# Seven half-size products for the gate, up and input tiles of a two-block transformer kernel, with the feed-forward values on token rows

## The chip, the cores and the metric

The kernel runs on one core of a Trainium2 chip. The metric is the device time of one execution in microseconds (us). TensorE (PE) multiplies matrices from SBUF into PSUM banks, VectorE (DVE) and ScalarE (ACT) work on the results, and SyncE (SP) issues the loads of weights. All data are fp32.

## The reference

256 tokens of width 1024 pass a first block (a Hyena and mLSTM mixer, then a 16-expert feed-forward) and two layers of a second block. The change is only in the second block, in these lines:

```
h = rms_norm(x, norm_mix[l]) * (1.0 + sc_m) + sh_m
(q_a, kc_a, ..., v_b, g_br) = jnp.split(h @ w_in[l], split_at, axis=-1)
...
h = rms_norm(x, norm_ffn[l]) * (1.0 + sc_f) + sh_f
gt, up = jnp.split(h @ w_ffn_in[l], 2, axis=-1)
x = x + g_f * ((jax.nn.silu(gt) * up) @ w_ffn_out[l])
```

`w_in` is 1024 x 4888, of which the first 2840 columns are projected to token rows; `w_ffn_in` is 1024 x 5632 (gate and up, 2816 each), `w_ffn_out` 2816 x 1024.

## The kernel before

The program is written out by hand, one instruction stream per engine, with semaphores between them. `step(name)` counts a finished instruction, `wait_ge(*at(name))` waits for it. Weights come as a stream of tiles, 128 partitions x 4096 floats (2 MB: 1024 rows x 512 columns), into a ring of four slots; the tile four places on is loaded as soon as TensorE has used the slot (`mark_used`, `one`). Six PSUM banks of 512 columns rotate (`bank`); a claim waits until the bank's last content is read.

Activations `h2` stand turned, channels on partitions: 8 blocks of 128 channels x 256 tokens. Two forms of a linear layer use them. `pe_linear_tok` (L837) holds 128 tokens of `h2` as the stationary side and streams 512 weight columns, 8 matmuls for each half of the tokens, so the result has tokens on partitions; the input projection `pe_in` uses it for six tiles (five of 512 columns, one of 280), and ScalarE copies each bank to `qkv` (`act_in`, L1826). `pe_linear_T` (L823) holds 128 weight columns and streams the 256 tokens, 8 matmuls for each of 4 column blocks, so the result stands turned. The feed-forward `pe_ffn` uses it for six gate and six up tiles (the sixth has 256 columns); ScalarE applies SiLU to gate banks (`act_ffn`, L2362), VectorE multiplies with up (`dve_ffn`, L2375) into `ffT`, which the down projection (L2342, 176 matmuls) streams.

A layer of the second block is, on TensorE: norm, `pe_late` (a vector product with two tiles of the next ada matrix, L633), `pe_in`, `pe_compress` with gate matmuls, attention, the mixer's output (L1375, then L823), norm, `pe_late`, `pe_ffn`. On VectorE, the norm's scaling (L744; L802 and L808 at the first layer, where two norms are joined) goes ahead of what the layer needs.

## Time and profile before

| | us |
|---|---|
| median of 3 runs | 2339.05 (2338.96 to 2340.21) |
| profiled execution | 2338.81 |
| its span, first to last instruction | 2337.0 |
| TensorE busy | 1974.4 (84%) |
| VectorE busy | 414.0 (18%) |
| ScalarE busy | 319.6 (14%) |

A busy share is an average over stages with different limits: the expert loop in the middle third waits for weights from HBM. The chain of waits says, for each moment, which work the end depended on. The trace holds two TensorE records for each fp32 matmul and one for a transpose.

### The profile page before, as it was taken

How to read it: one execution, taken by the hardware profiler on the slowest of the kernel's cores; microseconds unless marked ns; L12 is line 12 of the kernel's file. 1: busy time of each engine (PE TensorE's matmuls, PEld its weight loads, DVE VectorE, ACT ScalarE, POOL GpSimd, SP SyncE). 2: the span in 40 equal slices, each digit the busy share in tenths (PEclk: the TensorE clock that was granted, in tenths of full speed). 3: DMA queues.
4: the chain of work that ended last, by engine and by line, in shares of the span. 5: the costliest groups of instructions: out<-in, count | busy, mean ns of one | idle time of the engine just before them, and what ended most of it. 6: DMA issues, size and time to landing. Idle time of an engine off the chain costs nothing.

```text
span 2337.0 us, 27864 instructions
## 1 busy us (share of the span) xinstructions
PE 1974.4 (84%) x12006; PEld 1244.0 (53%) x12006; DVE 414.0 (18%) x1223; ACT 319.6 (14%) x724; POOL 0.2 (0%) x4
## 2 busy tenths in 40 slices
PE   7999999966666666666666689999999999999999
PEld 4468678521111111111111155878888748688888
DVE  5113334300000000000000032551000106620000
ACT  3132030200000000000000022341000103510000
POOL 0000000000000000000000000000000000000000
PEclk9999999988787888877788799999999999999999
DMA  9146568999999999999999973526434545255341
GB/s 350 71 147 221 208 241 307 403 428 428 429 428 429 428 429 428 429 428 429 428 429 429 429 283 129 210 80 234 162 108 162 200 162 198 85 187 188 119 180 36
DMA packets 147871, 648.45 MB, mean 277 GB/s; under 512 B 10645, under 2 KB 17410, under 8 KB 123016
## 3 DMA queue, kind: packets, MB, share of 16 engines
q1 hardware_dynamic: 143956, 643.74, 69.6%
q10 hardware_dynamic: 3828, 3.43, 0.5%
q8 instruction: 69, 1.13, 0.2%
q14 instruction: 18, 0.15, 0.0%
HBM read 646.10 MB, written 1.05 MB: 277 GB/s over the span
## 4 chain that ended last, share of the span: by engine, by line
PE 61%; DMA 33%; DVE 3%; ACT 1%; issue 1%; SPq 1%; ACTq 0%; DVEq 0%
DMA ring<-in_w_exp 32%; PE bank L823 26%; PE bank L837 7%; PE bank L2342 7%; PE bank L1623 4%; PE bank L1375 4%; PE bank L2302 2%; PE bank L1638 2%; PE bank L856 1%; DMA ring<-in_w_ada 1%; PE bank L593 1%; DVE scr L2213 1%; PE bank L633 1%; PE bank L1300 1%; PE bank L701 1%
## 5 line engine op out<-in xcount | busy, mean ns | idle before, releaser
L823 PE MATMUL bank<-hx,ring 128*128 128x256 f32 (+1 forms) x2688 | 600.0, 386 | 0.7 <-ACT hx L719 0.7
L823 PEld LDWEIGHTS bank<-hx,ring 128*128 128x128 f32 x2688 | 512.2, 191 | 86.9 <-issue 19.1
L1623 PE MATMUL bank<-ring,arena 128*32 128x512 f32 x1968 | 307.5, 759 | 203.0 <-DMA ring<-in_w_exp 192.6
L1623 PEld LDWEIGHTS bank<-ring,arena 128*32 128x32 f32 x1968 | 61.1, 124 | 432.7 <-DMA ring<-in_w_exp 312.6
L1638 PE MATMUL bank<-ring,arena 128*32 128x512 f32 x1008 | 162.6, 785 | 80.9 <-DMA ring<-in_w_exp 70.1
L2342 PE MATMUL bank<-arena,ring 128*128 128x256 f32 x704 | 152.4, 379 | 1.5 <-DVE arena L2375 1.5
L837 PE MATMUL bank<-ring,hx 128*128 128x512 f32 (+1 forms) x384 | 152.9, 561 | 0.7 <-ACT hx L779 0.7
L2342 PEld LDWEIGHTS bank<-arena,ring 128*128 128x128 f32 x704 | 133.7, 190 | 20.0 <-issue 1.9
L1638 PEld LDWEIGHTS bank<-ring,arena 128*32 128x32 f32 x1008 | 32.5, 131 | 194.3 <-DMA ring<-in_w_exp 114.6
L837 PEld LDWEIGHTS bank<-ring,hx 128*128 128x128 f32 x384 | 72.8, 190 | 79.6 <-issue 75.3
L1681 DVE COPY arena<-bank 128x256 f32<-128x256 f32 x16 | 6.8, 424 | 519.0 <-PE bank L1628 519.0
L1375 PE MATMUL bank<-arena,ring 128*128 128x256 f32 x384 | 85.3, 385 | 2.1 <-DVE arena L1264 2.1
L1375 PEld LDWEIGHTS bank<-arena,ring 128*128 128x128 f32 x384 | 73.9, 193 | 13.0 <-issue 2.7
L1688 DVE COPY arena<-bank 128x256 f32<-128x256 f32 x16 | 6.8, 424 | 348.5 <-PE bank L1512 348.5
L2375 DVE TENSOR_TENSOR arena<-bank,scr 128x512 f32<-128x512 f32 x22 | 15.2, 691 | 286.5 <-PE bank L823 286.5
L1646 PE MATMUL bank<-arena 128*128 128x256 f32 x256 | 59.8, 387 | 5.2 <-ACT arena L1667 5.2
L1646 PEld LDWEIGHTS bank<-arena 128*128 128x128 f32 x256 | 47.6, 191 | 19.6 <-issue 13.0
L2302 PE MATMUL bank<-hx,ring 128*128 128x256 f32 x256 | 57.3, 382 | 0.0
L1663 ACT COPY arena<-bank 128x512 f32<-128x512 f32 x16 | 9.4, 585 | 348.3 <-PE bank L1631 348.3
L2302 PEld LDWEIGHTS bank<-hx,ring 128*128 128x128 f32 x256 | 48.0, 190 | 8.2 <-issue 1.8
L2362 ACT ACTIVATE scr<-bank 128x512 f32<-128x512 f32 x22 | 13.1, 597 | 261.7 <-PE bank L823 261.6
L1661 ACT ACTIVATE arena<-bank 128x512 f32<-128x512 f32 x16 | 9.6, 597 | 279.0 <-PE bank L1623 279.0
(375 smaller groups left out, 1418.9 us busy)
## 6 DMA issues: line engine op xcount, KB each, us to landing
ring<-in_w_exp SPq DMA_DIRECT2D x186, 2048.0 KB, 16.2
ring<-in_w_ada SPq DMA_DIRECT2D x36, 2048.0 KB, 12.4
ring<-in_w_in SPq DMA_DIRECT2D x29, 2048.0 KB, 9.1
...
```

Source lines behind the costliest of these rows:

```text
L593: ins = pe.matmul(banks[6][32 * j:32 * j + 32, (i % 4) * P:(i % 4 + 1) * P], cT[:, k, :], w[:, k, j * P:(j + 1) * P], start=k == 0, stop=k ...
L633: ins = pe.matmul(b[32 * j:32 * j + 32, i * P:(i + 1) * P], cT[:, k, :], w[:, k, j * P:(j + 1) * P], start=k == 0, stop=k == KD - 1)
L701: ins = pe.matmul(b[:, 0:n], ones[:, 0:P], sq[:, k, :], start=k == 0, stop=k == KD - 1)
L823: ins = pe.matmul(b[:, o:o + n], w[:, k, j * P:(j + 1) * P], h[:, k, :], start=k == 0, stop=k == KD - 1)
L837: ins = pe.matmul(b[:, 0:n], h[:, k, c * P:(c + 1) * P], w[:, k, :], start=k == 0, stop=k == KD - 1)
L856: pe.matmul(b[:, :], hcx[:, k, s * N + c * P:s * N + (c + 1) * P], w[:, k, :], start=k == 0, stop=False)
L1375: ins = pe.matmul(b[:, s * N:(s + 1) * N], w[:, k, j * P:(j + 1) * P], y[:, k, :], start=k == 0, stop=k == 3)
L1623: ins = pe.matmul(banks[s][32 * j:32 * j + 32, :], e_xe[:, 2 * t + kk, :], w[:, kk, 512 * j:512 * j + 512], start=t + kk == 0, stop=t + kk ...
L1638: ins = pe.matmul(banks[half][32 * k:32 * k + 32, :], e_hT[:, k, 32 * t:32 * t + 32], w[:, k, 512 * half:512 * half + 512], start=t == 0, ...
L1646: ins = pe.matmul(banks[4 + j // 2][:, (j % 2) * N:(j % 2 + 1) * N], e_y[:, j * P:(j + 1) * P], e_G, start=False, stop=True, skip_group_ch ...
L2302: ins = pe.matmul(b[:, j * N:(j + 1) * N], w[:, k, (2 * i + j) * P:(2 * i + j + 1) * P], h2[:, k, :], start=k == 0, stop=k == KD - 1)
L2342: ins = pe.matmul(acc[j // 2][:, (j % 2) * N:(j % 2 + 1) * N], w[:, k, j * P:(j + 1) * P], ffT[:, f, :], start=f == 0 and j % 2 == 0, stop ...
```

## The change

A product of the 256 x 1024 activations with a 1024 x 512 weight tile is split in halves three ways (tokens, channels, columns). Instead of eight half-size products it makes seven, by the scheme of Winograd and Strassen: four sums of weight quarters (T1 to T4, VectorE, 128 x 1024 each, for every tile), four sums of activation parts (S1 to S4, once a layer for each use), seven products of 4 matmuls of 256 columns, and additions of the results (u2, u3, c22, c21, c12 on VectorE; a copy of m1 and of c11 on ScalarE). Tokens are on partitions in the result. This is done for input tiles 1, 3, 4 and 5 and for gate and up tiles 0 to 4 of each layer. In the feed-forward SiLU and product are made on token rows (`gtok`, `htok`), and eight transposes for each tile pair turn them for the down projection. The sixth, small pair of tiles keeps the old form and comes first.

```diff
@@ -291,7 +291,7 @@
         late_tiles(3 * l + 2)
         wf = A["w_ffn_in_2"][l]
         gt, up = wide(wf, 0, FF2), wide(wf, FF2, 2 * FF2)
-        for i in range(len(gt)):
+        for i in (5, 0, 1, 2, 3, 4):
             tiles2(f"gt{l}_{i}_", gt[i:i + 1])
             tiles2(f"up{l}_{i}_", up[i:i + 1])
         tiles2(f"down{l}_", deep(A["w_ffn_out_2"][l], 0, FF2))
@@ -1811,7 +1811,130 @@
     def pe_in(pe, l):
         PE.stage("second")
         for t in range(6):
-            pe_linear_tok(pe, f"in{l}_{t}", f"in{l}_{t}", h2, None if t else f"h mix{l + 1}")
+            if t in SEVEN:
+                pe_seven(pe, f"in{l}_{t}", f"in{l}_{t}", SEVEN.index(t) % 2, f"S in{l}")
+            else:
+                pe_linear_tok(pe, f"in{l}_{t}", f"in{l}_{t}", h2, None if t else f"h mix{l + 1}")
+
+    SEVEN = (1, 3, 4, 5)
+    tsum = view(arena, 7088, P, 2, 4, 1024)
+    ssum = view(arena, 15280, P, 4, 4, P)
+    m1, u2, u3 = scr[:, 2048:2304], scr[:, 2304:2560], scr[:, 2560:2816]
+
+    def quarter(w, kh, nh):
+        return w[:, 4 * kh:4 * kh + 4, 256 * nh:256 * nh + 256]
+
+    def part(th, kh):
+        return h2[:, 4 * kh:4 * kh + 4, th * P:(th + 1) * P]
+
+    def tsums(half):
+        return [tsum[:, half, i].rearrange("p (k n) -> p k n", k=4) for i in range(4)]
+
+    def pe_seven(pe, key, tkey, half, s_ready, between=None):
+        w = tile(pe, tkey)
+        T1, T2, T3, T4 = tsums(half)
+        S1, S2, S3, S4 = (ssum[:, i] for i in range(4))
+
+        def product(name, b, a, x, first):
+            for k in range(4):
+                ins = pe.matmul(b[:, 0:256], a[:, k, :], x[:, k, :], start=first and k == 0, stop=True, skip_group_check=True)
+            ins.then_inc(*PE.step(f"{name} {key}"))
+
+        r1 = bank(pe, f"{key}r1")
+        product("m1", r1, part(0, 0), quarter(w, 0, 0), True)
+        pe.wait_ge(*at(f"T2 {key}"))
+        pe.wait_ge(*at(s_ready))
+        r2 = bank(pe, f"{key}r2")
+        product("m6", r2, S2, T2, True)
+        if between:
+            between()
+        r3 = bank(pe, f"{key}r3")
+        product("m5", r3, S1, T1, True)
+        pe.wait_ge(*at(f"u2 {key}"))
+        product("m7", r2, S3, T3, False)
+        pe.wait_ge(*at(f"m1 copied {key}"))
+        product("m2", r1, part(0, 1), quarter(w, 1, 0), False)
+        pe.wait_ge(*at(f"T4 {key}"))
+        pe.wait_ge(*at(f"u3 {key}"))
+        product("m4", r2, part(1, 1), T4, False)
+        pe.wait_ge(*at(f"c22 {key}"))
+        product("m3", r3, S4, quarter(w, 1, 1), False)
+        mark_used(pe, tkey)
+
+    def dve_tsum(v, key, tkey, half, two_back, i):
+        w = tile(v, tkey)
+        T1, T2, T3, T4 = tsums(half)
+        if i == 0:
+            if two_back:
+                v.wait_ge(*at(f"m3 {two_back}"))
+            v.tensor_tensor(T1, quarter(w, 0, 1), quarter(w, 0, 0), ALU.subtract).then_inc(*DV.step(f"T1 {key}"))
+        elif i == 1:
+            v.tensor_tensor(T3, quarter(w, 1, 1), quarter(w, 0, 1), ALU.subtract).then_inc(*DV.step())
+        elif i == 2:
+            v.wait_ge(*at(f"T1 {key}"))
+            v.tensor_tensor(T2, quarter(w, 1, 1), T1, ALU.subtract).then_inc(*DV.step(f"T2 {key}"))
+        else:
+            v.wait_ge(*at(f"T2 {key}"))
+            v.tensor_tensor(T4, quarter(w, 1, 0), T2, ALU.subtract).then_inc(*DV.step(f"T4 {key}"))
+
+    def dve_ssum(v, ready, name):
+        v.wait_ge(*at(ready))
+        S1, S2, S3, S4 = (ssum[:, i] for i in range(4))
+        v.tensor_tensor(S1, part(1, 0), part(1, 1), ALU.add).then_inc(*DV.step())
+        s1 = DV.last()
+        v.tensor_tensor(S3, part(0, 0), part(1, 0), ALU.subtract).then_inc(*DV.step())
+        v.wait_ge(*s1)
+        v.tensor_tensor(S2, S1, part(0, 0), ALU.subtract).then_inc(*DV.step())
+        v.wait_ge(*DV.last())
+        v.tensor_tensor(S4, part(0, 1), S2, ALU.subtract).then_inc(*DV.step(name))
+
+    def dve_seven(v, key, tkey, half, after, before, out, gate=None):
+        b1, b2, b3 = (bank_of(f"{key}r{i}")[:, 0:256] for i in (1, 2, 3))
+
+        def gated(c, h):
+            if gate is not None:
+                v.wait_ge(*DV.last())
+                x = out(c, h)
+                v.tensor_tensor(x, x, gate[:, c, 256 * h:256 * h + 256], ALU.mult).then_inc(*DV.step(f"{key} gated"))
+
+        v.wait_ge(*at(f"m1 copied {key}"))
+        v.wait_ge(*at(f"m6 {key}"))
+        if before:
+            v.wait_ge(*at(f"{before} sums"))
+        v.tensor_tensor(u2, b2, m1, ALU.add).then_inc(*DV.step(f"u2 {key}"))
+        if after:
+            dve_tsum(v, *after, 0)
+            dve_tsum(v, *after, 1)
+        v.wait_ge(*at(f"m7 {key}"))
+        v.tensor_tensor(u3, b2, m1, ALU.add).then_inc(*DV.step(f"u3 {key}"))
+        v.wait_ge(*at(f"m5 {key}"))
+        v.wait_ge(*at(f"u3 {key}"))
+        v.tensor_tensor(out(1, 1), b3, u3, ALU.add).then_inc(*DV.step(f"c22 {key}"))
+        gated(1, 1)
+        if after:
+            dve_tsum(v, *after, 2)
+        if gate is not None:
+            v.wait_ge(*at(f"m2 {key}"))
+            v.tensor_tensor(out(0, 0), b1, gate[:, 0, 0:256], ALU.mult).then_inc(*DV.step(f"free {key}r1", f"{key} gated"))
+        if after:
+            dve_tsum(v, *after, 3)
+        v.wait_ge(*at(f"m4 {key}"))
+        v.tensor_tensor(out(1, 0), b2, m1, ALU.add).then_inc(*DV.step(f"free {key}r2", f"c21 {key}"))
+        gated(1, 0)
+        v.wait_ge(*at(f"m3 {key}"))
+        v.tensor_tensor(out(0, 1), b3, u2, ALU.add).then_inc(*DV.step(f"free {key}r3", f"{key} sums"))
+        gated(0, 1)
+
+    def dve_in_tiles(v, l):
+        DV.stage("second")
+        todo = [(f"in{l}_{t}", f"in{l}_{t}", n % 2, f"in{l}_{SEVEN[n - 2]}" if n >= 2 else None) for n, t in enumerate(SEVEN)]
+        for i in range(4):
+            dve_tsum(v, *todo[0], i)
+        dve_ssum(v, f"h mix{l + 1} done", f"S in{l}")
+        for n, t in enumerate(SEVEN):
+            lo = IN_COLS[t][0]
+            dve_seven(v, *todo[n][:3], todo[n + 1] if n < 3 else None, todo[n - 1][0] if n else None,
+                      lambda c, h: qkv[:, c, lo + 256 * h:lo + 256 * h + 256])
 
@@ -1819,12 +1942,23 @@
         AC.stage("second")
         act.wait_ge(*at("x moe" if l == 0 else "ffn read0"))
         for t, (lo, hi) in enumerate(IN_COLS):
+            if t in SEVEN:
+                key = f"in{l}_{t}"
+                b = bank_of(f"{key}r1")[:, 0:256]
+                act.wait_ge(*at(f"m1 {key}"))
+                if t != SEVEN[0]:
+                    act.wait_ge(*at(f"c21 in{l}_{SEVEN[SEVEN.index(t) - 1]}"))
+                act.copy(m1, b).then_inc(*AC.step(f"m1 copied {key}"))
+                act.wait_ge(*at(f"m2 {key}"))
+                act.copy(qkv[:, 0, lo:lo + 256], b).then_inc(*AC.step(f"free {key}r1", f"in{l} {t}"))
+                continue
             for c in range(NC):
                 key = f"in{l}_{t}{c}"
                 act.wait_ge(*at("full " + key))
                 b = bank_of(key)
                 act.copy(qkv[:, c, lo:hi], b[:, 0:hi - lo]).then_inc(*AC.step("free " + key, f"in{l} {t}"))
         act.wait_ge(*AC.last())
+        act.wait_ge(*at(f"in{l}_5 sums"))
         for c in range(NC):
             for col, H, lo, _ in GROUPS:
                 act.activation(sqh[:, c, lo * HD:(lo + H) * HD], qkv[:, c, col:col + H * HD], ACT.Square).then_inc(*AC.step(f"squares{l}"))
@@ -1879,6 +2013,7 @@
 
         PE.stage("compress")
         pe.wait_ge(*at(f"in{l} 1"))
+        pe.wait_ge(*at(f"in{l}_1 sums"))
         pe.wait_ge(*at("pe ready"))
         for s in range(2):
             key = f"cturn{l}{s}"
@@ -2324,18 +2459,38 @@
                                            b[:, :].rearrange("p (j t) -> p j t", j=2), ACT.Sigmoid).then_inc(*AC.step("free " + key, f"gates{l + 1}"))
 
 
+    gtok = view(arena, 17328, P, NC, 512)
+    htok = view(arena, 18352, P, NC, 512)
+
+    def pe_hidden_turn(pe, l, i):
+        pe.wait_ge(*at(f"u{l}{i} gated"))
+        for h in range(2):
+            b = bank(pe, f"turn{l}{i}{h}")
+            for j in range(2):
+                for c in range(NC):
+                    o = (j * NC + c) * P
+                    q = (2 * h + j) * P
+                    ins = pe.transpose(b[:, o:o + P], htok[:, c, q:q + P], ident[:, :])
+            ins.then_inc(*PE.step(f"full turn{l}{i}{h}"))
+
     def pe_ffn(pe, l):
         PE.stage("ffn")
-        for i in range(6):
-            nb = 4 if i < 5 else 2
-            pe_linear_T(pe, f"g{l}{i}_", f"gt{l}_{i}_0", h2, N, nb, None if i else f"h ffn{l + 1}")
-            pe_linear_T(pe, f"u{l}{i}_", f"up{l}_{i}_0", h2, N, nb)
+        pe_linear_T(pe, f"g{l}5_", f"gt{l}_5_0", h2, N, 2, f"h ffn{l + 1}")
+        pe_linear_T(pe, f"u{l}5_", f"up{l}_5_0", h2, N, 2)
+        for i in range(5):
+            pe_seven(pe, f"g{l}{i}", f"gt{l}_{i}_0", 0, f"S ffn{l}", (lambda: pe_hidden_turn(pe, l, i - 1)) if i else None)
+            pe_seven(pe, f"u{l}{i}", f"up{l}_{i}_0", 1, f"S ffn{l}")
         pe_late_turn(pe, 3 * l + 2)
         acc = [bank(pe, f"down{l}{i}") for i in range(4)]
         pe.wait_ge(*at(f"hidden{l}"))
+        pe.wait_ge(*at(f"turned{l}3"))
         for t in range(6):
             w = tile(pe, f"down{l}_{t}")
             nk = 4 if t < 5 else 2
+            if t == 1:
+                pe_hidden_turn(pe, l, 4)
+            if t == 4:
+                pe.wait_ge(*at(f"turned{l}4"))
             for j in range(KD):
                 for k in range(nk):
                     f = 4 * t + k
@@ -2351,30 +2506,64 @@
     def act_ffn(act, l):
         AC.stage("ffn")
         act.wait_ge(*at(f"h ffn{l + 1} done"))
+        act.wait_ge(*at(f"full g{l}5_0"))
+        act.activation(sg[:, 0, :], bank_of(f"g{l}5_0")[:, :], ACT.Silu).then_inc(*AC.step(f"free g{l}5_0", f"sg{l}"))
+
+        def turns(i):
+            for h in range(2):
+                key = f"turn{l}{i}{h}"
                 act.wait_ge(*at("full " + key))
+                f = 4 * i + 2 * h
+                act.copy(ffT[:, f:f + 2, :].rearrange("p a b -> p (a b)"), bank_of(key)[:, :]).then_inc(
+                    *AC.step("free " + key, f"turned{l}{i}"))
+
+        for i in range(5):
+            for x in "gu":
+                key = f"{x}{l}{i}"
+                act.wait_ge(*at(f"m1 {key}"))
+                last = f"u{l}{i - 1}" if x == "g" else f"g{l}{i}"
+                if i or x == "u":
+                    act.wait_ge(*at(f"c21 {last}"))
+                b = bank_of(f"{key}r1")[:, 0:256]
+                act.copy(m1, b).then_inc(*AC.step(f"m1 copied {key}"))
+                if x == "u":
+                    continue
+                if i:
+                    turns(i - 1)
+                    act.wait_ge(*at(f"{last} gated"))
+                act.wait_ge(*at(f"m2 {key}"))
+                act.activation(gtok[:, 0, 0:256], b, ACT.Silu).then_inc(*AC.step(f"free {key}r1"))
+                act.wait_ge(*at(f"c21 {key}"))
+                act.activation(gtok[:, 1, :], gtok[:, 1, :], ACT.Silu).then_inc(*AC.step())
+                act.wait_ge(*at(f"{key} sums"))
+                act.activation(gtok[:, 0, 256:512], gtok[:, 0, 256:512], ACT.Silu).then_inc(*AC.step(f"silu{l}{i}"))
+        turns(4)
 
     def dve_ffn(v, l):
         DV.stage("ffn")
+        todo = []
+        for i in range(5):
+            for n, (x, w) in enumerate((("g", "gt"), ("u", "up"))):
+                todo.append((f"{x}{l}{i}", f"{w}{l}_{i}_0", n, f"{x}{l}{i - 1}" if i else None))
+        for i in range(4):
+            dve_tsum(v, *todo[0], i)
+        dve_ssum(v, f"h ffn{l + 1} done", f"S ffn{l}")
+        v.wait_ge(*at(f"full u{l}5_0"))
+        v.wait_ge(*at(f"sg{l}"))
+        v.tensor_tensor(ffT[:, 20:22, :].rearrange("p a b -> p (a b)"), bank_of(f"u{l}5_0")[:, :], sg[:, 0, :],
+                        ALU.mult).then_inc(*DV.step(f"free u{l}5_0", f"hidden{l}"))
+        for n, item in enumerate(todo):
+            i, up = n // 2, n % 2
+            after = todo[n + 1] if n + 1 < len(todo) else None
+            if up:
+                v.wait_ge(*at(f"silu{l}{i}"))
+                if i:
+                    v.wait_ge(*at(f"full turn{l}{i - 1}1"))
+            elif i:
+                v.wait_ge(*at(f"u{l}{i - 1} gated"))
+            dst = htok if up else gtok
+            dve_seven(v, *item[:3], after, todo[n - 1][0] if n else None,
+                      lambda c, h: dst[:, c, 256 * h:256 * h + 256], gtok if up else None)
         dve_late(v, 3 * l + 2)
         DV.stage("ffn")
         v.wait_ge(*at(f"ada21 part{3 * l + 2}"))
@@ -2525,6 +2714,7 @@
             if l == 0:
                 v.memset(kct, 0.0).then_inc(*DV.step())
                 v.memset(sC, 0.0).then_inc(*DV.step())
+            dve_in_tiles(v, l)
             dve_blocks(v, l)
             dve_late(v, 3 * l)
             dve_in(v, l)
```

TensorE's order in the feed-forward of a layer, from the late tiles' vector product to the norm that follows. Before:

```order
247 L633 MATMUL bank<-ring,small 32x128 x64
248 L823 MATMUL bank<-hx,ring 128x256 x352
249 L645 MATMUL bank<-ident,arena 128x128 x2
250 L2342 MATMUL bank<-arena,ring 128x256 x176
251 L701 MATMUL bank<-scr,ones 128x256 x8
```

Now, up to the first turn (L1840 is the product in `pe_seven`, L823 the small tiles; `hx` holds `h2`, `arena` the sums):

```order
267 L823 MATMUL bank<-hx,ring 128x256 x32
268 L1840 MATMUL bank<-ring,hx 128x256 x4
269 L1840 MATMUL bank<-arena 128x256 x12
270 L1840 MATMUL bank<-ring,hx 128x256 x4
271 L1840 MATMUL bank<-arena,hx 128x256 x4
272 L1840 MATMUL bank<-ring,arena 128x256 x4
273 L1840 MATMUL bank<-ring,hx 128x256 x4
274 L1840 MATMUL bank<-arena 128x256 x12
275 L1840 MATMUL bank<-ring,hx 128x256 x4
276 L1840 MATMUL bank<-arena,hx 128x256 x4
277 L1840 MATMUL bank<-ring,arena 128x256 x4
278 L1840 MATMUL bank<-ring,hx 128x256 x4
```

One run of 352 matmuls became 32 and then 28 for each of ten tiles; from the second pair on, 8 transposes (L2473) stand behind the gate tile's second product, and the last 8 behind 32 matmuls of the down projection.

VectorE's order at the first layer's input projection, from the end of the joined norm. Before:

```order
294 L2527 MEMSET arena 128x512
295 L1974 TENSOR_TENSOR hx<-bank,arena 64x256 x8
296 L661 TENSOR_TENSOR ada<-bank,cols 128x8
297 L1843 TENSOR_TENSOR arena<-arena 128x256
298 L1845 SCALAR_TENSOR_TENSOR arena<-arena 128x4x32
```

Now, up to the third result addition (L1870 to L1878 are T1, T3, T2, T4; L1883 to L1889 the activation sums; L1904 is u2, L1909 u3):

```order
294 L2716 MEMSET arena 128x512
295 L1870 TENSOR_TENSOR arena<-ring 128x1024
296 L1872 TENSOR_TENSOR arena<-ring 128x1024
297 L1875 TENSOR_TENSOR arena<-ring,arena 128x1024
298 L1878 TENSOR_TENSOR arena<-ring,arena 128x1024
299 L1883 TENSOR_TENSOR arena<-hx 128x512
300 L1885 TENSOR_TENSOR arena<-hx 128x512
301 L1887 TENSOR_TENSOR arena<-arena,hx 128x512
302 L1889 TENSOR_TENSOR arena<-hx,arena 128x512
303 L1904 TENSOR_TENSOR scr<-bank,scr 128x256
304 L1870 TENSOR_TENSOR arena<-ring 128x1024
305 L1872 TENSOR_TENSOR arena<-ring 128x1024
```

VectorE, which had nothing to do between the norm and the compression's block sums (L1974), has sums ahead of the first seven-product tile and the next tile's sums between the result additions.

## Rows read from the trace of the kernel before

**Rows 1.** the page, busy us of each engine, its share of the span, instructions
```profile
PE 1974.4 (84%) x12006; PEld 1244.0 (53%) x12006; DVE 414.0 (18%) x1223; ACT 319.6 (14%) x724; POOL 0.2 (0%) x4
```

**Rows 2.** the chain of waits in order of time: start us, us, what
```profile
1370.59 76.45 PE bank L837 x192
...
1617.53 152.20 PE bank L823 x704
...
1770.69 76.21 PE bank L2342 x352
...
1854.61 76.41 PE bank L837 x192
...
2100.82 152.20 PE bank L823 x704
```

**Rows 3.** busy us by stretch, instructions; then granted clock, DMA share, GB/s
```profile
core 0: us, PE busy (x) PEld busy (x) DVE busy (x) ACT busy (x) POOL busy (x), PEclk, DMA share, GB/s
450.00:1350.00 900.00, 584.33 (x3622) 171.00 (x3612) 39.55 (x93) 39.65 (x77) 0.00 (x0) 0.82 1.00 427
1488.00:1550.00 62.00, 57.91 (x425) 41.43 (x422) 41.33 (x207) 37.71 (x129) 0.00 (x0) 0.97 0.28 104
1972.00:2034.00 62.00, 57.15 (x428) 40.66 (x426) 41.41 (x207) 38.31 (x130) 0.00 (x0) 1.00 0.29 104
1617.00:1770.00 153.00, 152.59 (x714) 134.01 (x706) 9.77 (x18) 11.28 (x21) 0.00 (x0) 1.00 0.47 165
1371.00:1447.00 76.00, 76.00 (x194) 36.38 (x193) 7.25 (x16) 8.85 (x19) 0.00 (x0) 1.00 0.47 163
```

**Rows 4.** ScalarE in order of time in the first input projection
```profile
1384.60 0.58 ACT L1826 COPY arena<-bank 128x512 f32<-128x512 f32 x1 [6.23 <-PE bank L837]
1391.47 0.58 ACT L1826 COPY arena<-bank 128x512 f32<-128x512 f32 x1 [6.28 <-PE bank L837]
1398.33 0.58 ACT L1826 COPY arena<-bank 128x512 f32<-128x512 f32 x1 [6.28 <-PE bank L837]
```

**Rows 5.** TensorE's transposes of heads in order of time
```profile
1484.98 2.82 PE L2034 MATMUL bank<-ident,arena 128*128 128x128 f32 x24
1487.64 1.04 PE L2034 MATMUL bank<-ident,hx 128*128 128x128 f32 x8
```

**Rows 6.** TensorE at the first down projection, and the chain there
```profile
1770.69 76.21 PE L2342 MATMUL bank<-arena,ring 128*128 128x256 f32 x352 [0.76 <-DVE arena L2375]
...
1769.75 0.70 DVE arena L2375
1770.45 0.24 issue
```

**Rows 7.** VectorE and ScalarE by line and form: xcount | busy us, mean ns
```profile
L2375 DVE TENSOR_TENSOR arena<-bank,scr 128x512 f32<-128x512 f32 x22 | 15.2, 691 | 286.5 <-PE bank L823 286.5
...
L1864 DVE TENSOR_TENSOR arena<-arena 128x256 f32<-128x256 f32 x12 | 5.0, 416 | 0.1
...
L808 DVE SCALAR_TENSOR_TENSOR xT<-xT,cols,scr 128x256 f32<-128x256 f32 x8 | 3.3, 480 | 0.0
...
L494 DVE TENSOR_TENSOR arena<-mg 128x512 f32<-128x512 f32 x4 | 2.7, 686 | 0.0
...
L1256 DVE TENSOR_TENSOR arena<-arena,small 128x1024 f32<-128x1024 f32 x1 | 1.2, 1226 | 0.0
...
L2362 ACT ACTIVATE scr<-bank 128x512 f32<-128x512 f32 x22 | 13.1, 597 | 261.7 <-PE bank L823 261.6
...
L1941 ACT COPY arena<-bank 128x256 f32<-128x256 f32 x2 | 0.7, 372 | 2.7 <-PE bank L1903 2.7
```

**Rows 8.** TensorE where the second layer's gate tiles end, in order of time
```profile
1931.95 27.79 PE L823 MATMUL bank<-hx,ring 128*128 128x256 f32 x128
1959.67 1.09 PE L1903 MATMUL bank<-ring,hx 128*32 128x128 f32 x29
```

**Rows 9.** VectorE ahead of the first input projection's end, and at the second's start
```profile
1375.37 3.26 DVE L808 SCALAR_TENSOR_TENSOR xT<-xT,cols,scr 128x256 f32<-128x256 f32 x8
...
1378.75 0.48 DVE L2527 MEMSET arena<- 128x512 f32 x1
...
1853.16 3.26 DVE L744 SCALAR_TENSOR_TENSOR scr<-xT,small,rs 128x256 f32<-128x256 f32 x8
```

**Rows 10.** weight loads issued at the first feed-forward's start, and the queue's rate
```profile
1615.50 0.37 SPq L2554 DMA_DIRECT2D ring<-in_w_ffn_in  x1
...
1620.00:1621.00 1.00, 1.00 (x6) 0.90 (x5) 0.00 (x0) 0.43 (x2) 0.00 (x0) 1.00 1.04 406
1621.00:1622.00 1.00, 1.00 (x7) 0.87 (x6) 0.00 (x0) 0.00 (x0) 0.00 (x0) 1.00 1.05 406
```

More of the change, by code:

```diff
@@ L2365, in dve_ffn @@
+        turns(4)
     def dve_ffn(v, l):
         DV.stage("ffn")
-        n = 0
-        for i in range(6):
-            for j in range(2 if i < 5 else 1):
-                key = f"u{l}{i}_{j}"
-                v.wait_ge(*at("full " + key))
-                b = bank_of(key)
-                v.wait_ge(*at(f"sg{l}_{n}"))
-                f = 4 * i + 2 * j
-                v.tensor_tensor(ffT[:, f:f + 2, :].rearrange("p a b -> p (a b)"), b[:, :], sg[:, n % 2, :],
-                                          ALU.mult).then_inc(*DV.step("free " + key, f"hid{l}_{n}", f"hidden{l}"))
-                n += 1
+        todo = []
```

9 lines of the change are left out of this document (removed).

## The prediction

> **What bounds the kernel now.** I read the page's busy shares first [rows 1]: TensorE 84%, VectorE 18%, ScalarE 14%. A share over the whole run says nothing of one stage, so next comes the chain of waits in order of time [rows 2]. After the expert loop it runs nearly unbroken through TensorE: 76.45 and 76.41 us in the two input projections (L837, 96 matmuls each), 152.20 us in each feed-forward gate/up stage (L823, 352 matmuls), 76.21 us in each down projection. The trace keeps two records for each fp32 matmul, so x704 is 352 matmuls. The third view, busy time by stretch [rows 3], shows TensorE at 76.00 of 76 us in the first input projection and 152.59 of 153 us in the first feed-forward, with VectorE at 7.25 and 9.77 us, and a DMA share of 0.47. Here only TensorE's work and what it waits for count. The change is wholly in these stages.
>
> **TensorE's work removed.** A 512-column gate or up tile costs 32 matmuls of 256 columns; each takes 152.20 / 352 = 0.432 us [rows 2], so 13.84 us. Seven products of 4 such matmuls are 28, or 12.11 us. Five gate and five up tiles save 40 matmuls: 17.30 us a layer. An input tile costs 16 matmuls of 512 columns; the copies behind each bank of 8 start 6.87 us apart [rows 4], so 13.73 us. Its 28 half-width matmuls again cost 12.11 us: 1.62 saved, 6.48 for four tiles. Here the matmuls nearly double in number (16 to 28); that is already inside 0.432, read from a stream of just this form.
>
> **TensorE's work added.** The hidden values now stand on token rows, so each of five tile pairs needs 8 transposes. In a run of 24 the next group starts 2.66 us after the first, 0.111 each [rows 5]: 40 are 4.44 us a layer, all in TensorE's stream and counted in full (the last eight stand inside the down projection).
>
> **A wait that goes.** Before the down projection TensorE sat 0.76 us until the last VectorE multiply [rows 6]. That multiply now belongs to the small tile, done first; the last turned tile is needed only at down tile 4. I credit 0.76 a layer.
>
> **New waits.** Every product but m1 and m5 starts behind at least one semaphore of VectorE or ScalarE. I laid one tile out from TensorE's start, 1.73 us a product. m6 ends at 3.46; VectorE adds m1 into u2, about 0.42 [rows 7] (the 256-wide row; of the 512-wide ones one takes 0.691 from a bank and one 0.686 from SBUF), and TensorE sees it 0.24 later, the issue time after a VectorE step [rows 6]: ready at 4.2, wanted by m7 at 5.19. Then two weight sums of the next tile, 1.23 each [rows 7], fill VectorE to 6.4, before m7 ends at 6.92; u3 is visible at 7.6, wanted by m4 at 8.65; c22 at 8.1, wanted by m3 at 10.4. The ScalarE copy of m1 (0.37 us [rows 7]) is ready at 2.3, wanted by u2 at 3.5. The smallest slack is 1.0 us. VectorE's sum is 4 x 1.23 + 5 x 0.42 = 7.0 us in a gate or input tile and four more small operations, 8.7, in an up tile, so 15.7 against TensorE's 25.1 with the turns. The SiLU of the gate tile stands in three pieces on ScalarE, none over the 0.60 us of a 512-wide one [rows 7], the last after m3; VectorE wants it 3.5 us into the up tile. The turn of tile i-1 stands two products into gate tile i, when the gating (two operations after m3, 0.9 us) is over. Queued behind these waits on VectorE are the next tile's sums; they have a whole tile of slack.
>
> What does a satisfied wait cost? The old gate/up stream claims a bank behind a wait every 16 matmuls and shows no gap; the change of tile at L823 to L1903 bounds it: 64 matmuls from 1931.95 should end at 1959.62 and the next starts at 1959.67 [rows 8], 0.05. There are 28 products a layer in the input and 70 in the feed-forward, 196 in all. So the bounds are 0 and 196 x 0.05 = 9.8 us. I take 0, by the nearest row, the stream of the same shape.
>
> **The starts.** In layer 0, VectorE is busy until 1379.2 with the old normalisation and two clears [rows 9], so the four sums of input tile 1 and the four of the activations come after it. Independent VectorE operations start 0.07 before the one ahead ends (eight L808 of 0.480 in 3.26), dependent ones don't: 4 x 1.23 - 0.14 = 4.8 and 4 x 0.69 - 0.14 = 2.6, ending at 1386.6. TensorE starts at 1370.59 [rows 2], ends tile 0 at 1384.3 and m1 at 1386.05; with the 0.24 it waits 0.8 us. Layer 1 has no such tail: VectorE is free at 1856.4, TensorE wants the sums at 1870. In the feed-forward the first seven-product tile is loaded into the slot freed by the first late tile: the issue is at 1615.50 [rows 10], and the queue moves a 2 MB tile in 5.3 us at about 400 GB/s [rows 10], behind a 1 MB one, so it lands by 1622.9. Sums end at 1630.3, and TensorE, with 13.9 us of small tiles from 1617.53 and one product, wants them at 1633.1. Nothing lost, 2.8 us of slack. At the other ends nothing changes hands later: the ScalarE squares behind the input projection wait for one 0.42 us add instead of a 0.58 us copy, and 27 us of gate matmuls cover that chain.
>
> **Sum.** A layer: 6.48 + 17.30 - 4.44 + 0.76 = 20.1. Two layers less 0.8: 39.4. The profiled execution took 2338.81 us (span 2337.0 and 1.8 around it), 0.24 below the median; 2338.8 - 39.4 = 2299.4, and on the median's footing 2299.6 us, 1.7% less.
>
> **A rule against it.** TensorE's granted clock is 1.00, the 2.4 GHz level, in all these stretches [rows 3]; in the attention stretch, where 57.91 of 62 us are busy and scores, turns and values wait for other engines all the time, it is 0.97 and 1.00, and in the expert loop, where it is busy 584 of 900 us, 0.82. The Trainium skill (TensorE: Matmul & The Clock Gate, "A second HAM failure mode: psum-queue depth-cycling") warns that cycling through PSUM banks with micro-idles between groups of matmuls makes the clock swing between its two levels; three banks a tile with seven hand-overs is that pattern. The attention row speaks against it as long as slack holds. If it did happen as in the expert loop, 28 seven-product tiles of 12.11 us, 339 us, at 0.82 would cost 74 us more: 2374.
>
> **Rivals and chances.**
> - Forecast: products run back to back. 76%. Its own range 2296 to 2304, for the starts' small waits and the transposes.
> - Part-paid hand-overs: each of 196 products loses the 0.05 of rows 8, because its weight load isn't drawn ahead over a wait. 2309. For it: most product starts are now behind a wait satisfied only 1 us before. Against: no gap at the old bank claims. 13%.
> - The sums come late at the four phase starts, by up to their whole length of 7.4 us each: 29 us back, 2329. For it: the weight sums need the tile a whole tile earlier than TensorE did, and the DMA share near a start is 1.0 [rows 10]. Against: the times above. 4%.
> - The other side: each product pays the whole 0.24 us [rows 6] from wait to first matmul, because one hand-over in the ring m6-u2-m7-u3-m4-c22-m3 is slower than laid out and the rest follow. 196 x 0.24 = 47 us, more than the 39.4 saved: 2347. The point where it decides is 0.20 us a product. For it: the dependent pieces alternate between two engines and one m1 buffer serves all tiles. Against: 1.0 us of slack at the tightest. 4%.
> - The clock swings as in the expert loop: 2374. 3%.
> That the multiplications don't become fewer is excluded: the order of the program has them.
>
> The range: 2295 to 2316. Below it I know of no gain; above, it holds the part-paid case and some. Faster by over 0.2% (4.7 us, about what a measurement of this kernel can tell from no change): 92%, the first three cases less a little; within 0.2%: 1%; slower: 7%, the last two.
>
> **What would show it.** Each seven-product tile in the changed profile should take 12.1 us, 60.5 for a run of five; TensorE's matmul time in gate/up 134.9 plus 4.4 a layer; the idle time of TensorE before products near zero save 0.8 us at m6 of the first input tile; VectorE's busy time at most 414 + 2 x (9 x 7.0 + 5 x 8.7), 627 us; the granted clock at 1.00. Wrong it would be if VectorE rows named as releasers stand before the product line in long sums, or if the pitch of the 256-column matmuls rises above 0.432.

## The result, and the profile after

| | before | after |
|---|---|---|
| median, us | 2339.28 (2338.96 to 2340.21) | 2299.48 (2298.65 to 2299.87) |
| profiled execution, its span | 2338.81, 2337.0 | 2299.32, 2297.5 |
| ratio | | 0.9829, 95% interval 0.9813 to 0.9845 |

1.7% less, 39.8 us, where 39.4 was forecast. The page of the changed kernel, its busy line (busy us, share of the span, instructions) and the first line of the chain that ended last:

```profile
PE 1937.0 (84%) x12118; PEld 1257.2 (55%) x12118; DVE 614.3 (27%) x1511; ACT 336.7 (15%) x774; POOL 0.2 (0%) x4
PE 60%; DMA 33%; DVE 4%; ACT 1%; issue 1%; ACTq 0%; SPq 0%; DVEq 0%
```

Against [rows 1], TensorE lost 37.4 us of busy time and VectorE gained 200. VectorE's gain stands nowhere in the time; the next views show why. The chain of waits of the changed kernel in order of time (start us, us, what):

```profile
1386.27 10.60 PE bank L1840 x48
1396.87 7.55 PE bank L837 x32
1404.42 36.26 PE bank L1840 x168
...
1611.64 14.05 PE bank L823 x64
1625.69 27.63 PE bank L1840 x128
...
1654.19 24.18 PE bank L1840 x112
```

L1840 is the line of the seven products, L823 here the small old-form tiles, L837 here the 280-column tile. Three seven-product tiles are one piece of 36.26 us, 12.09 a tile, with no other engine between them; [rows 2] has 76.45 and 152.20 us for the same stages. Between the last two pieces stand 0.87 us of turns, the transposes of the hidden values. Per record it is 24.18 / 112 = 0.216, so 0.432 us from one matmul's start to the next: the old stream's pitch.

The stretches of the changed kernel (busy us and instructions of PE, PEld, DVE, ACT, POOL, granted clock, DMA share, GB/s), two of the changed stages' and two out of attention (the last two rows, which the part on the prediction takes up):

```profile
1371.00:1441.00 70.00, 69.74 (x292) 54.70 (x292) 36.27 (x55) 7.46 (x19) 0.00 (x0) 1.00 0.51 177
1612.00:1750.00 138.00, 138.00 (x657) 121.67 (x656) 79.07 (x118) 19.60 (x42) 0.00 (x0) 1.00 0.55 196
...
1514.00:1516.00 2.00, 2.00 (x14) 1.35 (x12) 0.87 (x4) 0.52 (x2) 0.00 (x0) 0.50 0.01 2
...
1978.00:1980.00 2.00, 2.00 (x12) 1.38 (x11) 0.55 (x2) 1.11 (x3) 0.00 (x0) 0.50 0.00 0
```

In both stages TensorE is busy all but 0.26 us, as in [rows 3], at the granted clock 1.00, the 2.4 GHz level. VectorE now works 79 of 138 us where it worked 9.77 of 153.

Stage by stage, from TensorE's first matmul of one to that of the next, in us (an input projection is counted up to the matmuls at L823, with 1.1 us of small transposes behind its last tile):

| stage | before | after | change | forecast |
|---|---|---|---|---|
| start of the first input projection | 1370.59 | 1370.32 | -0.27 | 0 |
| input projection 1 | 77.38 | 71.29 | -6.09 | -5.7 |
| to feed-forward 1 (attention, mixer) | 169.56 | 170.03 | +0.47 | 0 |
| gate and up 1 | 153.16 | 138.48 | -14.68 | -14.5 |
| down 1 to input projection 2 | 83.85 | 84.45 | +0.60 | +0.9 |
| input projection 2 | 77.41 | 70.79 | -6.62 | -6.5 |
| to feed-forward 2 | 168.87 | 169.83 | +0.96 | 0 |
| gate and up 2 | 153.17 | 138.47 | -14.70 | -14.5 |
| down 2 to TensorE's end | 79.15 | 79.96 | +0.81 | +0.9 |

The sum is -39.5. The two gate/up stages carry 32 of the 40 turns and the wait that went; the last eight turns are in the down rows.

Next the ring of hand-overs (m6, u2, m7, u3, m4, c22, m3) that the prediction laid out by hand; `ring` in the rows is something else, the four weight slots. TensorE's timeline in the changed kernel (start us, us, what, then idle time and releaser in brackets), the first input tiles, a later seven-product tile up to m2, a place in attention (for later), m6 of the first gate tile, and turns:

```profile
1370.32 13.97 PE L837 MATMUL bank<-ring,hx 128*128 128x512 f32 x32 [0.73 <-ACT hx L779]
1384.12 1.89 PE L1840 MATMUL bank<-ring,hx 128*128 128x256 f32 x8
1386.27 5.42 PE L1840 MATMUL bank<-arena 128*128 128x256 f32 x24 [0.26 <-DVE arena L1889]
1391.53 1.89 PE L1840 MATMUL bank<-ring,hx 128*128 128x256 f32 x8
...
1404.26 1.89 PE L1840 MATMUL bank<-ring,hx 128*128 128x256 f32 x8
1405.98 5.34 PE L1840 MATMUL bank<-arena 128*128 128x256 f32 x24
1411.16 1.89 PE L1840 MATMUL bank<-ring,hx 128*128 128x256 f32 x8
...
1511.91 1.00 PE L2225 MATMUL bank<-ident,scr 128*128 128x128 f32 x6 [2.34 <-DVE scr L2371]
1512.84 1.55 PE L2240 MATMUL bank<-scr,arena 128*64 128x256 f32 x8
1514.32 1.12 PE L2280 MATMUL bank<-ident,arena 128*128 128x128 f32 x4
...
1627.26 5.34 PE L1840 MATMUL bank<-arena 128*128 128x256 f32 x24
...
1653.16 1.04 PE L2473 MATMUL bank<-ident,arena 128*128 128x128 f32 x8
```

VectorE's timeline there, around the first tile's m6 and at the feed-forward's start:

```profile
1385.48 0.69 DVE L1889 TENSOR_TENSOR arena<-hx,arena 128x512 f32<-128x512 f32 x1
1388.35 0.42 DVE L1904 TENSOR_TENSOR scr<-bank,scr 128x256 f32<-128x256 f32 x1 [2.17 <-PE bank L1840]
1388.69 1.22 DVE L1870 TENSOR_TENSOR arena<-ring 128x1024 f32<-128x1024 f32 x1
1389.82 1.22 DVE L1872 TENSOR_TENSOR arena<-ring 128x1024 f32<-128x1024 f32 x1
1391.73 0.42 DVE L1909 TENSOR_TENSOR scr<-bank,scr 128x256 f32<-128x256 f32 x1 [0.69 <-PE bank L1840]
...
1617.79 1.23 DVE L1870 TENSOR_TENSOR arena<-ring 128x1024 f32<-128x1024 f32 x1 [4.06 <-DMA ring<-in_w_ffn_in]
...
1624.45 0.69 DVE L1889 TENSOR_TENSOR arena<-hx,arena 128x512 f32<-128x512 f32 x1
...
1629.26 0.42 DVE L1904 TENSOR_TENSOR scr<-bank,scr 128x256 f32<-128x256 f32 x1 [2.83 <-PE bank L1840]
```

The first m6 was due at 1384.12 + 8 x 0.216 = 1385.85; the activation sums ended at 1386.17 and it started at 1386.27, 0.42 late. Then u2 (L1904) ended at 1388.77, 0.96 us ahead of m7, which was due two products (16 x 0.216) behind m6, at 1389.73. The next tile's first two sums were over at 1391.04, and VectorE stood idle 0.69 us until m7 let u3 (L1909) go: in this ring VectorE waits for TensorE. What TensorE waited for at L1840 over the whole run (us, times):

```profile
  issue: 1.0, 4
  DVE arena L1889: 0.9, 2
```

0.9 us is that one wait, counted on the matmuls and again on the weight loads. No other releaser stands there for 28 tiles and 196 products.

### The profile page after: what moved, and what is told of

Its sections match the earlier page's. It is cut to its first block, busy times and chain, and to the rows that moved or that the text cites. A ratio compares the mean times of both kernels' runs of the same rounds, so it can differ in the third digit from the quotient of the medians.

```text
span 2297.5 us, 28642 instructions
## 1 busy us (share of the span) xinstructions
PE 1937.0 (84%) x12118; PEld 1257.2 (55%) x12118; DVE 614.3 (27%) x1511; ACT 336.7 (15%) x774; POOL 0.2 (0%) x4
## 4 chain that ended last, share of the span: by engine, by line
PE 60%; DMA 33%; DVE 4%; ACT 1%; issue 1%; ACTq 0%; SPq 0%; DVEq 0%
DMA ring<-in_w_exp 32%; PE bank L1840 15%; PE bank L823 14%; PE bank L2497 7%; PE bank L1623 4%; PE bank L1375 4%; PE bank L2437 2%; PE bank L1638 2%; PE bank L837 1%; PE bank L856 1%; PE bank L701 1%; DVE scr L2348 1%; PE bank L593 1%; PE bank L1300 1%; PE bank L1309 1%
## 5 line engine op out<-in xcount | busy, mean ns | idle before, releaser
L823 PE MATMUL bank<-hx,ring 128*128 128x256 f32 (+1 forms) x1408 | 323.5, 391 | 0.7 <-ACT hx L719 0.7
L823 PEld LDWEIGHTS bank<-hx,ring 128*128 128x128 f32 x1408 | 268.6, 191 | 54.2 <-issue 19.4
L1840 PE MATMUL bank<-arena 128*128 128x256 f32 x672 | 151.0, 379 | 0.3 <-DVE arena L1889 0.3
L1840 PEld LDWEIGHTS bank<-arena 128*128 128x128 f32 x672 | 127.0, 190 | 17.5 <-DVE arena L1889 0.6
L1840 PE MATMUL bank<-ring,hx 128*128 128x256 f32 x448 | 105.8, 379 | 0.0
L1840 PEld LDWEIGHTS bank<-ring,hx 128*128 128x128 f32 x448 | 85.1, 190 | 12.5 <-issue 1.0
L1646 PE MATMUL bank<-arena 128*128 128x256 f32 x256 | 59.7, 386 | 5.2 <-ACT arena L1667 5.2
L1646 PEld LDWEIGHTS bank<-arena 128*128 128x128 f32 x256 | 47.6, 191 | 19.6 <-issue 13.0
L1840 PE MATMUL bank<-arena,hx 128*128 128x256 f32 x224 | 52.9, 379 | 0.0
L1840 PE MATMUL bank<-ring,arena 128*128 128x256 f32 x224 | 52.9, 379 | 0.0
## 6 DMA issues: line engine op xcount, KB each, us to landing
ring<-in_w_ada SPq DMA_DIRECT2D x36, 2048.0 KB, 12.2
```

Of the source, the lines that this page charges most:

```text
L823: ins = pe.matmul(b[:, o:o + n], w[:, k, j * P:(j + 1) * P], h[:, k, :], start=k == 0, stop=k == KD - 1)
L1646: ins = pe.matmul(banks[4 + j // 2][:, (j % 2) * N:(j % 2 + 1) * N], e_y[:, j * P:(j + 1) * P], e_G, start=False, stop=True, skip_group_ch ...
L1840: ins = pe.matmul(b[:, 0:256], a[:, k, :], x[:, k, :], start=first and k == 0, stop=True, skip_group_check=True)
```

## The experiments

**Halves alone.** The forecast rests on the two parts being independent terms. In the first kernel `pe_ffn`, `act_ffn` and `dve_ffn` are those of before, and the loads' order too:

```diff
-        for i in (5, 0, 1, 2, 3, 4):
+        for i in range(len(gt)):
```

In the second `pe_in` and `act_in` take the old branch for every tile, and the two waits for the tiles' sums are gone:

```diff
-            if t in SEVEN:
+            if t in ():
...
-            dve_in_tiles(v, l)
```

> Seven products in input tiles 1, 3, 4, 5 alone; the feed-forward as before. If TensorE's work is all that counts, a layer saves 4 x (13.73 - 12.09) = 6.56 us and the first one loses the 0.42 us wait at its second product: 12.7 us less than before, 2326.5. If the hand-overs cost something that the feed-forward happened to hide, less is saved: at 0.05 us for each of 56 products, 9.9 us, 2329.4.

> Seven products in gate and up tiles 0 to 4 alone; the input projection as before. By TensorE's work a layer saves 40 x 0.432 = 17.3, pays 40 transposes at 0.109 (4.4) and saves the 0.76 us wait ahead of the down projection: 27.4 us less than before, 2311.9. The two halves then add up to the whole, 12.7 + 27.4 = 40.1 against 39.8 measured. If they share a cost or hide one for each other, the sum of the two differs from the whole by more than 1.5 us.

Input only: 2326.83 (2326.46 to 2327.45), ratio 0.9946 (0.9927 to 0.9965), the stages 71.28 and 70.79 us, gate/up 153.16 as before. Feed-forward only: 2309.34 (2309.02 to 2310.21), ratio 0.9871 (0.9852 to 0.989), gate/up 138.48 twice, the input stages 77.38. Against before's 2338.3 on that chip the two gain 11.5 and 29.0, together 40.4, where the whole change gains 39.8: they add. The stages say it more exactly: those that each half changes take the same time as in the whole change, to 0.01 us. The second is 2.6 below its expectation; 1.4 of it is an earlier start of the first input projection (1369.14), in a stage that neither kernel changes. The chain of the first around its one wait:

```profile
1384.85 0.70 DVE arena L1889
1385.55 0.09 issue
1385.64 10.60 PE bank L1840 x48
```

From VectorE's end to TensorE's start it is 0.09 here, not the 0.24 of [rows 6].

**No weight sums.** Does VectorE's work beside TensorE cost anything? This kernel leaves the weight sums out and multiplies the quarters as loaded. The edit:

```diff
-        if i == 0:
-            if two_back:
-                v.wait_ge(*at(f"m3 {two_back}"))
...
+        return
...
-        pe.wait_ge(*at(f"T2 {key}"))
-        T1, T2, T3, T4 = tsums(half)
+        T1, T2, T3, T4 = quarter(w, 0, 1), quarter(w, 1, 1), quarter(w, 0, 1), quarter(w, 1, 0)
```

> The four sums of weight quarters on VectorE are left out, with the waits for them; the products take the quarters as loaded (so the result is not the sums' product). VectorE loses 136 us of work that reads the ring beside TensorE. If that work is wholly beside TensorE's, only the first layer's wait at the second product goes: 0.4 us less, 2299.1. If reading the ring from two engines, or the waits, slow TensorE, the matmul pitch falls under 0.432 us and the time by more than 2 us.

2297.22 (2296.24 to 2299.69), ratio 0.9821 (0.9801 to 0.9841); input stages 70.79 twice, gate/up 138.48. A stretch of its feed-forward:

```profile
1623.00:1748.00 125.00, 125.00 (x598) 110.36 (x597) 29.67 (x70) 15.17 (x33) 0.00 (x0) 1.00 0.49 176
```

VectorE's share fell from over a half to a quarter, and TensorE's gate/up stage is the same to 0.01 us. 28 x 4 sums of 1.22 us, 136 us of work, cost TensorE nothing but the start: the first input stage is 0.50 shorter, the wait at m6 with what follows it. The median is 1.9 below its expectation; 1.7 of that stands ahead of the first input projection (1368.66 against 1370.32), where the kernels are the same.

**No turns.** The edit, on TensorE (ScalarE's copies and the waits for them go too, and the down projection reads values that nobody wrote):

```diff
-            pe_seven(pe, f"g{l}{i}", f"gt{l}_{i}_0", 0, f"S ffn{l}", (lambda: pe_hidden_turn(pe, l, i - 1)) if i else None)
+            pe_seven(pe, f"g{l}{i}", f"gt{l}_{i}_0", 0, f"S ffn{l}", None)
...
-            if t == 1:
-                pe_hidden_turn(pe, l, 4)
```

> The 80 transposes of the hidden values and their copies are left out, with the waits for them (the down projection then reads values that nobody wrote). If they cost their TensorE time alone, 80 x 0.109 = 8.7 us go: 2290.8. If their stand between two products also delays the ring of hand-overs, more goes, up to 2 us a pair: 2281.

2289.55 (2289.07 to 2293.12), ratio 0.9783 (0.9767 to 0.9799). Its chain in the feed-forward:

```profile
1628.25 120.87 PE bank L1840 x560
```

Ten tiles unbroken, 134.97 us from the first small tile to the down projection (138.48 with turns), and the down stage 83.58 (84.45): 3.51 + 0.87 = 4.38 us a layer, 0.109 a transpose. The forecast had 4.44. So a layer's turns cost TensorE their own time and the ring nothing; the 2281 of the other expectation falls.

**u2 behind the sums.** The ring's slack was the main step. Here u2 comes after two weight sums, so that it must be late:

```diff
-        v.tensor_tensor(u2, b2, m1, ALU.add).then_inc(*DV.step(f"u2 {key}"))
         if after:
             dve_tsum(v, *after, 0)
             dve_tsum(v, *after, 1)
+        v.tensor_tensor(u2, b2, m1, ALU.add).then_inc(*DV.step(f"u2 {key}"))
```

> The addition u2 stands behind the next tile's first two weight sums on VectorE. Laid out from the trace of the changed kernel: m6 ends 3.46 us into a tile, the two sums take 2.3 more, u2 0.42, TensorE sees it 0.1 to 0.24 later, at 6.4 against 5.18 wanted by m7: 1.2 us lost in each of 16 tiles without turns that have a next tile, 0.35 in the 8 with turns: 22 us, 2321.5. If late hand-overs cost more than their lateness (the whole ring slips, or the granted clock leaves 1.00), the loss is over 30 us; if the queue of TensorE hides them, under 10.

2327.17 (2325.78 to 2329.47), ratio 0.9945 (0.9929 to 0.9962): 28.3 us lost in the four stages, more than expected. TensorE's timeline in the second seven-product tile, then VectorE's:

```profile
1406.54 3.62 PE L1840 MATMUL bank<-arena 128*128 128x256 f32 x16
1411.27 1.99 PE L1840 MATMUL bank<-arena 128*128 128x256 f32 x8 [1.12 <-DVE scr L1907]
```
```profile
1408.52 1.22 DVE L1870 TENSOR_TENSOR arena<-ring 128x1024 f32<-128x1024 f32 x1 [10.63 <-PE bank L1840]
1410.80 0.42 DVE L1907 TENSOR_TENSOR scr<-bank,scr 128x256 f32<-128x256 f32 x1
```

m7 was due at 1406.54 + 16 x 0.216 = 1409.99 and started at 1411.27, 0.05 behind u2's end: 1.28 late. Its eight records then take 1.99 us where an undelayed product takes 1.89. So a late hand-over costs its lateness and 0.10 more. I had expected neither that nor the 0.25 us by which VectorE's sums began behind m6 (it ends by its pitch at 1406.54 + 1.73 = 1408.27). Such waits, 0.34 to 1.31 us, stand in 24 of the 28 tiles, and the granted clock is 1.00 in all four stages. In the feed-forward the turns cover part: a pair of tiles takes 27.23 us against 25.05. The releaser L1907 now leads TensorE's idle list, as the prediction said a failed ring would show.

**Weight sums made twice and three times.** How far is VectorE from being the bound? Each sum is repeated, the repeat waiting for the one ahead:

```diff
-            v.tensor_tensor(T1, quarter(w, 0, 1), quarter(w, 0, 0), ALU.subtract).then_inc(*DV.step(f"T1 {key}"))
+            for r in range(2):
+                if r:
+                    v.wait_ge(*DV.last())
+                v.tensor_tensor(T1, quarter(w, 0, 1), quarter(w, 0, 0), ALU.subtract).then_inc(*DV.step(f"T1 {key}"))
```

T3, T2 and T4 likewise, and `range(3)` in the other kernel.

> Each weight sum is made twice, the second behind the first. u3 then ends 9.3 us into a tile and m4 wants it at 8.64: about 0.7 us lost in 16 tiles, nothing in the 8 with turns; VectorE's sum stays at the tile's length (11.8 and 13.5 us by 25.1 a pair), so nothing else is late: 11 us, 2310.5. If VectorE were already the bound of a tile, 24 x 4.9 = 118 us would come on top.

> Each weight sum is made three times. VectorE needs 12 x 1.3 + 2.1 = 17.7 us in a gate or input tile and 19.4 in an up tile, against TensorE's 12.1 and 12.5: VectorE is the bound of each tile that has a next one. Loss: in the input 3 x 5.6 a layer, in the feed-forward 4 x (37.1 - 25.1) and 5.6 for the last gate tile, and some 7 us at each start of the first layer's sums: 2 x 77 = 155 us, 2455, slower than before the change. By the hand-over lateness alone (u3 at 12.1 against 8.64, 3.4 us in 24 tiles) it would be 82 us: 2381.

Twice: 2333.22 (2329.84 to 2340.03), ratio 0.997 (0.996 to 0.998), far above the expected 2310.5. Three times: 2466.24 (2463.75 to 2467.97), ratio 1.0541 (1.0524 to 1.0559), slower than before the change and 11 above the expected 2455; a pair takes 36.15 us. Of the one with three, a stretch of the feed-forward, and what TensorE waited for at L1840:

```profile
1704.00:1834.00 130.00, 105.14 (x443) 87.26 (x442) 118.00 (x135) 10.65 (x25) 0.00 (x0) 0.92 0.32 113
```
```profile
  DVE scr L1921: 150.2, 48
```

There VectorE is the bound (118 of 130 us) and u3 (L1921) the releaser of 24 of the 28 m4s (each is counted on the matmuls and on the weight loads). With two the engines are level: the forecast's 15.7 us a pair and 8 more sums of 1.22 are 25.5, against 25.05 of TensorE, and a pair takes 26.71. TensorE in the kernel with two, then stretches at two of its starts:

```profile
1388.48 8.13 PE L1840 MATMUL bank<-arena 128*128 128x256 f32 x24 [5.29 <-DVE arena L1901]
...
1635.47 7.11 PE L1840 MATMUL bank<-arena 128*128 128x256 f32 x24 [2.62 <-DVE arena L1901]
...
1664.85 1.09 PE L2485 MATMUL bank<-ident,arena 128*128 128x128 f32 x8 [0.46 <-DVE arena L1910]
...
1683.96 1.96 PE L1840 MATMUL bank<-arena,hx 128*128 128x256 f32 x8 [0.75 <-DVE scr L1921]
```
```profile
1388.00:1392.00 4.00, 3.52 (x8) 2.86 (x9) 0.38 (x1) 0.00 (x0) 0.00 (x0) 0.50 0.12 45
...
1635.00:1639.00 4.00, 3.53 (x10) 2.92 (x11) 1.46 (x4) 0.00 (x0) 0.00 (x0) 0.66 0.91 333
```

My expectation had the lateness of u3 at m4 (0.75 in the last row, 0.7 expected in 16 tiles) and missed two things: the four sums ahead of each stage's first seven-product tile now take some 5 us more, and TensorE waits for them at three of the four starts (5.29, 2.62 and 2.57 us; not at the second input projection); and the gating falls behind and delays the turn (0.46). With the waits of 5.29 and 2.62 us the granted clock fell to 0.50, the 1.2 GHz level, so that the three products behind them took 8.13 and 7.11 us where they take 5.34.

**Twice, but not at the starts.** To tell long waits from the many short ones, the first tile of each stage has its sums once:

```diff
-            for r in range(2):
+            for r in range(1 if key in ("in0_1", "in1_1", "g00", "g10") else 2):
```

> Each weight sum made twice but for the first seven-product tile of each stage, so that the four starts are as in the changed kernel. If the loss of the run with all sums twice is lateness at m4 (0.9 us a tile without turns), at the turns (0.6) and, at the starts, waits of 2.6 to 5.3 us with a fall of TensorE's granted clock behind them, then the fall does not occur here and 2 x (2.5 + 6.9) = 19 us are lost: 2318.5. If the clock falls because of the many short waits, it falls here too and the loss stays near 31 us: 2330.

2321.05 (2317.05 to 2321.13), ratio 0.9915 (0.99 to 0.9931). Two of its stretches, and TensorE's idle time at L1840:

```profile
1370.00:1448.00 78.00, 75.19 (x381) 58.58 (x370) 55.16 (x76) 10.61 (x27) 0.00 (x0) 1.00 0.49 168
1612.00:1760.00 148.00, 142.15 (x777) 122.76 (x776) 123.99 (x157) 19.91 (x45) 0.00 (x0) 1.00 0.53 188
```
```profile
  DVE scr L1921: 27.5, 32
```

32 entries are 16 short waits (each on the matmuls and on the weight loads), and the clock stays at 1.00. The four stages lose 2.5, 7.6, 2.5 and 7.8 us, 20.4 together, where 19 were expected (34.4 with the starts' sums doubled too, so the starts cost about 14); the median is 2.6 above 2318.5, with a first input projection that starts 2.4 later than in the changed kernel's profile. The low clock of the kernel before this one came with the long waits at the starts, not with the many short ones.

**A fifth input tile.** Tile 0 is a 512-column tile that the change left in the old form because its sums would be wanted too early. Here the small tile 2 goes first, covering them, and the old normalisation's tail (`dve_final`, L808 of before) moves on VectorE behind the first tiles, and the two clears (L2715, L2716) behind the last. The tile order is the same for loads, TensorE and ScalarE:

```diff
-    SEVEN = (1, 3, 4, 5)
+    SEVEN = (0, 1, 3, 4, 5)
...
-        for t in range(6):
+        for t in (2, 0, 1, 3, 4, 5):
...
+            if l == 0 and n < 3:
+                dve_final(v, n)
```

> A fifth input tile (tile 0) with seven products; the 280-column tile goes first in the old form and covers the sums; VectorE's final normalisation of x is split into pieces behind the first three tiles. By TensorE's work: 1.64 us a layer less, and the first layer's 0.42 us wait shrinks to 0.1: 3.5 us less than the changed kernel, 2296.0. The rival: the small tile covers only 7.6 us against 7.3 us of sums (T and S), so TensorE waits at the second product of tile 0 in one or both layers; if the tile's weights land late by 2 us in each, the gain is eaten and the time stays at 2299.

It was run again, in five rounds, beside the changed kernel on the same chip:

> The changed kernel once more, on the chip that the next run uses: 2299.5 us by all theories, give or take 1.5 for the expert loop, whose end differed by up to 3 us between the runs so far.

> Five input tiles with seven products, against the changed kernel on the same chip. By the stages of its first profile (the two input projections 1.97 and 1.01 us shorter) it is 3.0 us faster: 2296.5. If the 5 to 6 us of the first look came from the change itself and not from the expert loop (1.0 us) and the clock in the second attention stretch (0.9 us), it is 5 us faster: 2294.5.

First 2293.52 (2291.55 to 2294.55), ratio 0.98 (0.978 to 0.9819), then 2294.0 (2292.22 to 2297.72), ratio 0.9808 (0.9794 to 0.9821); the changed kernel again 2298.23 (2296.47 to 2298.79), ratio 0.9824 (0.9811 to 0.9838). So this version is 4.2 us better than the changed one, between the 3.0 and the 5 of the two expectations. Its chain in the first input projection, and TensorE's timeline at the place in attention shown above:

```profile
1369.81 7.79 PE bank L840 x32
1377.60 60.61 PE bank L1843 x280
```
```profile
1509.44 0.98 PE L2231 MATMUL bank<-ident,scr 128*128 128x128 f32 x6 [2.33 <-DVE scr L2377]
1510.35 0.87 PE L2246 MATMUL bank<-scr,arena 128*64 128x256 f32 x8
1511.15 0.65 PE L2286 MATMUL bank<-ident,arena 128*128 128x128 f32 x4
```

Five tiles, 60.61 us: 280 records at 0.216 would be 60.5, and the rest is the first m6, 0.10 late (0.1 expected). In the second layer it is 0.10 late as well, in this kernel's first profile 0.55. The input stages take 69.33 and 69.32, 3.4 us less in all than the changed kernel's. Between the profiles of the last two (spans 2294.7 and 2291.4) stand also 2.4 us less in attention and 2.6 more before the first input projection, so that 3.4 of the 4.2 is what the changed stages show.

## Why the prediction was right

**TensorE's pitch.** The term rested on an old stream of the same shape: 0.432 a matmul, 12.11 a tile. Measured 0.432 and 12.09. The seven hand-overs cost nothing: the rival of part-paid hand-overs (9.8 us) falls, since three tiles stand as one piece of 36.26 us and ten, without turns, as one of 120.87.

**The ring's slack.** u2 was laid out ready 4.2 us into the tile (its terms, 3.46 + 0.42 + 0.24, add up to 4.12), wanted at 5.19. In the first tile it ended 0.96 ahead of need. In the first gate tile, which nothing delays, it ended at 1629.68: 4.15 us behind the tile's start (1625.53) and 1.04 ahead of m7. The number came right by two errors that cancel, which is luck: VectorE started 0.27 us behind m6's end by its pitch (1628.99), where the layout had nothing, and the hand-over back took 0.05 to 0.10, where it had 0.24. Moving it behind two sums gave late products at once, so the slack of about 1 us is real and small, as said. The rival of a price at every product (2347) falls because only one product in 196 waited; a ring late once a tile, u2 behind the sums, costs 28 us.

**VectorE.** At most 627 us was forecast, 614.3 came. Its sums beside TensorE cost nothing, shown by the kernel without them. Its reserve is smaller than the 27% of its busy line suggests: doubling the sums of all but each stage's first seven-product tile cost 20 us, tripling all made the kernel slower than before.

**Turns.** 4.44 forecast, 4.38 measured.

**Starts.** At the first input tile 0.8 us of wait were forecast, 0.42 came. Counted from TensorE's start the sums ended at 15.85 us (forecast 16.0), the product was due at 15.53 (15.46), and the hand-over took 0.10 where I took 0.24. Why it is 0.24 in that row, ahead of the down projection, no run here shows. In the second layer and at both feed-forwards no wait stands, as forecast. At the feed-forward VectorE had the tile 6.15 us behind TensorE's start and its sums ended at 1625.14; m6 was due at 1611.64 + 13.89 + 1.73 = 1627.26. So the slack was 2.1 us where 2.8 was written, the tile having landed 0.8 later into the stage than reckoned.

**The clock.** In the changed stages it was 1.00 throughout. The Trainium skill's warning (TensorE: Matmul & The Clock Gate, "A second HAM failure mode: psum-queue depth-cycling") did not come true here: three banks with seven hand-overs a tile kept 1.00, even with a short wait in 24 of 28 tiles (u2 behind the sums; the page's case is bf16 matmuls of 512 columns). With waits of 2.62 and 5.29 us it did fall to 0.50.

**What was not foreseen.** Attention became 1.43 us longer. In the timelines the six transposes at L2225 follow a 2.34 us wait for VectorE; in the changed kernel the clock then falls to 0.50 in both layers, and the eight records behind (L2240) take 1.55 us in the first, where the five-tile kernel has 0.87 after the same wait. From TensorE's starts that stretch of attention takes 44.23 us undisturbed, 45.39 and 45.18 in the changed kernel, 44.92 and 44.23 in the kernel before. That accounts for the +0.47 and +0.96 of the table. Why the clock falls after that wait in one run and not in another stays open. Of the down row's +0.60, 0.87 are turns and -0.20 a step from the ada product to the input projection that took 4.25 us in before's profile alone and 4.05 in all others; I don't know why, nor where the last 0.07 is.

So the input's 12.2 came as 12.7, the feed-forward's 27.2 with turns and the wait as 28.0, less 1.4 in attention and with 0.3 in the expert loop. That the median is 0.1 from the forecast is partly luck: +1.3 and +0.3 stand against -1.4, and the first start moves by several us from run to run (1367.2 to 1374.1 in these profiles).
